# Expert weights in one ring of nine places, and token rows fetched by index lists and transposed, in a four-layer diffusion backbone with mixtures of experts

## The reference

```
def moe(h, router_w, router_b, wg, wu, wd):
    x = h.reshape(B * T, D)
    scores = sigmoid(x @ router_w)
    ...                                   # group-limited top 2 of 16 per token
    combine = einsum('nk,nke->ne', w, one_hot(idx, N_EXPERTS))
    hid = silu(einsum('nd,edf->nef', x, wg)) * einsum('nd,edf->nef', x, wu)
    y = einsum('nef,efd->nd', hid * combine[..., None], wd)
```

## Time and profile before

| | us |
|---|---|
| median of 3 runs | 1986.24 |
| lowest and highest | 1983.18, 1988.86 |
| the profiled execution | 1988.12 |
| its span, first to last instruction | 1986.3 |

### The profile page before, as it was taken

The page is one execution under the profiler, slowest core; times in us unless marked ns, Lnnn a source line. Parts: engine busy times, 40 slices in busy tenths (PEclk is TensorE's granted clock), DMA queues, the critical chain, the costliest instruction groups (busy, mean ns, idle before and its releaser), DMA issues.

```text
span 1986.3 us, 22833 instructions
## 1 busy us (share of the span) xinstructions
PE 1845.2 (93%) x9280; PEld 1115.4 (56%) x9280; DVE 482.3 (24%) x1240; ACT 385.8 (19%) x801; POOL 12.3 (1%) x24
## 2 busy tenths in 40 slices
PE   4988999999999969999999997999999969999986
PEld 2656644545735858745445565844554748444543
DVE  0132511104300341411112434321112143311102
ACT  1132200003102660200002223200002142000002
POOL 1000000000000000000000000000000000000000
PEclk8998999999998988999999998999999989999988
DMA  9992599996997332579998884559999445599960
GB/s 328 350 401 80 212 397 427 428 419 242 356 359 259 117 122 91 215 311 428 428 427 311 321 292 170 215 216 425 428 429 401 140 193 211 233 424 429 427 265 22
DMA packets 126142, 593.34 MB, mean 299 GB/s; under 512 B 8008, under 2 KB 15312, under 8 KB 101088
## 3 DMA queue, kind: packets, MB, share of 16 engines
q1 hardware_dynamic: 115728, 585.12, 74.0%
q10 hardware_dynamic: 9840, 6.51, 1.1%
q0 software_dynamic: 480, 0.39, 0.1%
HBM read 587.28 MB, written 4.73 MB: 298 GB/s over the span
## 4 chain that ended last, share of the span: by engine, by line
PE 70%; DMA 18%; DVE 5%; ACT 4%; issue 2%; ACTq 1%; SPq 0%; DVEq 0%
PE PS L865 23%; PE PS L1358 18%; DMA ring<-in_moe_wu 16%; PE PS L1337 7%; PE PS L1369 7%; PE PS L894 3%; PE PS L914 2%; PE PS L1317 1%; DMA ring<-in_attn_w_qkv 1%; DMA ring<-in_w_mod 1%; PE PS L932 1%; ACT arena L594 1%; DVE RS L1495 1%; PE PS L1254 1%; PE PS L1322 1%
## 5 line engine op out<-in xcount | busy, mean ns | idle before, releaser
L1358 PE MATMUL PS<-ring,arena 128*64 128x512 f32 x1312 | 353.0, 595 | 4.8 <-DMA ring<-in_moe_wu 3.1
L1337 PE MATMUL PS<-arena 128*128 128x128 f32 (+3 forms) x1584 | 252.1, 317 | 10.8 <-ACT arena L800 4.4
L1337 PEld LDWEIGHTS PS<-arena 128*128 128x128 f32 (+1 forms) x1584 | 222.7, 195 | 52.5 <-issue 25.0
L800 ACT ACTIVATE arena<-PS 128x512 f32<-128x512 f32 (+2 forms) x131 | 71.3, 545 | 873.2 <-PE PS L1369 359.3
L865 PE MATMUL PS<-HS,ring 128*128 128x256 f32 x1024 | 233.8, 386 | 3.5 <-DVE HS L1565 1.6
L1369 PE MATMUL PS<-ring,arena 128*64 128x512 f32 x1024 | 226.8, 595 | 3.4 <-DVE arena L1822 3.4
L865 PEld LDWEIGHTS PS<-HS,ring 128*128 128x128 f32 x1024 | 194.8, 193 | 39.0 <-issue 10.0
L1358 PEld LDWEIGHTS PS<-ring,arena 128*64 128x64 f32 x1312 | 114.4, 137 | 159.6 <-issue 158.4
L1841 DVE TENSOR_TENSOR arena<-arena,PS 128x512 f32<-128x512 f32 x32 | 33.5, 1047 | 556.6 <-PE PS L1358 556.6
L865 PE MATMUL PS<-arena,ring 128*128 128x256 f32 (+1 forms) x672 | 147.6, 381 | 2.7 <-ACT arena L608 1.5
L1369 PEld LDWEIGHTS PS<-ring,arena 128*64 128x64 f32 x1024 | 70.7, 137 | 135.7 <-issue 127.9
(11 more groups left out here) (309 smaller groups left out, 1393.8 us busy)
## 6 DMA issues: line engine op xcount, KB each, us to landing
ring<-in_moe_wd SPq DMA_DIRECT2D x64, 2048.0 KB, 12.2
ring<-in_moe_wu SPq DMA_DIRECT2D x49, 2048.0 KB, 22.1
ring<-in_w_mod SPq DMA_DIRECT2D x48, 2048.0 KB, 16.1
ring<-in_moe_wg SPq DMA_DIRECT2D x33, 2048.0 KB, 19.7
arena<-in_moe_wg SPq DMA_DIRECT2D x32, 2048.0 KB, 20.8
HS<-in_moe_wu SPq DMA_DIRECT2D x16, 2048.0 KB, 28.4
ring<-in_mlstm_w_in SPq DMA_DIRECT2D x12, 2048.0 KB, 8.8
ring<-in_attn_w_qkv SPq DMA_DIRECT2D x6, 2048.0 KB, 20.1
```

The costliest lines, as they stand in the source:

```text
L800: A(dst, src, func).then_inc(S(sem), 1)
L1337: return mm(out, rows, onehot, start=first, stop=final, skip_group_check=True)
L1358: ins = mm(PS[64 * e:64 * e + 64, b, :], XG[:, k, 64 * e:64 * e + 64], w[:, k], start=(k == 0), stop=(k == KD - 1))
```

## The change

Places. The nine places (six of the ring, three of EXTRA) are now one first-in first-out ring for the experts' chunks: `plan_slots` gives each chunk its place, SLOT, and the chunk that was there before, BEHIND. Chunk q of a layer (0 to 47) goes to the place of chunk q - 9 and waits for its use. Chunks 3 to 8 are loaded into `ring` during the mixer; chunks 0 to 2 go to the spare places in arena and HS when the mixer's result is there. The mixers' chunks stay in the ring of six.

Rows. Once the tokens are turned into HT, ScalarE writes HT to HBM (HR, "token_rows", 256 x 1024). VectorE compares the ranks with the 64 places for pairs 1 to 7 at once (`onehot`), and 14 matmuls of one column (`slot_id`, between the two up products of pair 0) multiply that by the token numbers: a list of 128 token numbers for each pair, IDX. GpSimd fetches the rows of each pair by its list with an indirect DMA from HR into HT[:, p % 2], where HT is now a buffer of two; TensorE transposes them (`turn_x`, 8 transposes) where it multiplied. The token numbers are kept less 300 (`tid`) and 300 is added to the sum, so a place without a token has the number 300, which is out of bounds (255 is the last row): its row is not fetched. Pair 0 keeps the product gather. After the gather of pair 7 SP reads HR back into HT for the overflow's gather, and the mixers wait for that (semaphore back).

TensorE's loop is written out, the one-hot blocks PB are made for pair 0 and the overflow alone, and the semaphores of the overflow are merged into three.

```
+SPARE = 3
+def plan_slots():
+    slot, behind, count, last, loads, ring = [], [], [], {}, {}, 0
+    for n, (kind, l, _) in enumerate(CHUNKS):
+        q = n - POS["wg", l, 0] if kind in ("wg", "wu", "wd") else None
+        if q is not None and q < SPARE:
+            at = RING + q
+        elif q is not None and q >= RING + SPARE:
+            at = slot[n - RING - SPARE]
+        else:
+            at, ring = ring % RING, ring + 1
...
# SP
-                for j in range(6):
-                    load(n + j)
+                for q in range(SPARE, SPARE + RING):
+                    load(n + q)
                 sp.wait_ge(S("x"), KD * (2 * l + 2))
...
-                for j in range(6):
-                    if j == 2:
+                for q in range(SPARE):
+                    if q == SPARE - 1:
                         sp.wait_ge(S("ht"), 4 * (l + 1))
-                    weight(j, 1, 1, 0)
-                with sp.Fori(1, NPAIR // 2) as i:
-                    for par in range(2):
-                        for j in range(6):
-                            weight(j, 2 * i + par, par, i)
+                    load(n + q)
+                for q in range(SPARE + RING, 3 * NE):
+                    load(n + q)
                 n += 3 * NE
+                sp.wait_ge(S("gather"), 2 * NPAIR * (l + 1))
+                for s in range(2):
+                    sp.dma_start(HT[:, s], HR[P * s:P * s + P]).then_inc(S("back"), 16)
# GpSimd
+            def rows(l):
+                pool.wait_ge(S("idx"), l + 1)
+                pool.wait_ge(S("rows"), 32 * (l + 1))
+                for p in range(1, NPAIR):
+                    pool.wait_ge(S("gather"), 2 * NPAIR * l + 2 * max(p - 1, 1))
+                    pool.indirect_dma_start(HT[:, p % 2], None, HR, bass.IndirectOffsetOnAxis(IDX[:, p:p + 1], 0),
+                                            bounds_check=N2 - 1, oob_is_err=False).then_inc(S(f"slot_rows{p % 2}"), 16)
# ScalarE, after the copies of the turned tokens
+                    if b % 2:
+                        load(HR[P * (b // 2):P * (b // 2) + P], HT[:, b // 2], "rows")
# TensorE
+                def turn_x(banks, par, sem):
+                    for k in range(KD):
+                        ins = tp(bank(banks[k // 4], P * (k % 4), P * (k % 4) + P), HT[:, par, P * k:P * k + P], ident)
+                def slot_id():
+                    pe.wait_ge(S("onehot"), 2 * (l + 1))
+                    for p in range(1, NPAIR):
+                        for s in range(2):
+                            ins = mm(bank(3, p, p + 1), OH[:, s, p].rearrange("t y n -> t (y n)"), c_("tid")[:, s:s + 1], start=(s == 0), stop=(s == 1))
...
                         turn_w(here[1], "turn_w")
-                        gather(there, "gather")
+                        pe.wait_ge(S(f"slot_rows{1 - par}"), 8 * i + (48 * l + 8 if par else 64 * l + 16))
+                        turn_x(there, 1 - par, "gather")
# VectorE, after the weights of pair 1, and after the table EXI
+                onehot(0)
+                onehot(1)
...
+                v.wait_ge(S("slot_id"), l + 1)
+                idf = RT[:, 480:480 + NPAIR - 1]
+                go(ts(idf, bank(3, 1, NPAIR), 300.0, None, ALU.add))
+                go(v.tensor_copy(IDX[:, 1:NPAIR], idf), "idx")
```

More of the change, by code:

```diff
@@ L146 @@
 POS = {chunk: n for n, chunk in enumerate(CHUNKS)}
+SPARE = 3
[9 more added lines that the diff above has]
+            at, ring = ring % RING, ring + 1
+        slot.append(at)
+        behind.append(last.get(at))
+        loads[at] = loads.get(at, 0) + 1
+        count.append(loads[at])
+        last[at] = n
+    return slot, behind, count
+SLOT, BEHIND, LOADS = plan_slots()
 WARM = (8, 8, 3, 1)
@@ L417, in load @@
                     sp.wait_ge(S("load_x"), 32)
-                if n >= RING:
-                    wait(sp, *used(n - RING))
-                sp.dma_start(slot_view(kind, n % RING), src_of(kind, l, c)).then_inc(S(f"landed{n % RING}"), 16)
+                if BEHIND[n] is not None:
+                    wait(sp, *used(BEHIND[n]))
+                sp.dma_start(slot_view(kind, SLOT[n]), src_of(kind, l, c)).then_inc(S(f"landed{SLOT[n]}"), 16)
             n = 0
@@ L462, in _ @@
                 with sp.If(nx > 0):
-                    wait(sp, *used(n - 12))
-                    wait(sp, *used(n - 11))
-                    wait(sp, *used(n - 6))
+                    for j in range(3):
+                        wait(sp, *used(n - RING - SPARE + j))
                     with sp.Fori(0, nx) as i:
@@ L820, in moe @@
                 wts(n0, 0, 2)
-                pair(n0, 0)
+                pair(n0, 0, first=True)
                 pair(n0 + 1, 1)
@@ L842, in _ @@
                 affine(2 * l, l, 0)
+                wait(act, "back", 32 * l)
                 (lambda: attention(l // 3, l), mlstm, gla)[l % 3]()
@@ L848, in _ @@
             norm(2 * DEPTH)
+            act.wait_ge(S("back"), 32 * DEPTH)
             for k in range(KD):
@@ L1909, in moe @@
+                        v.wait_ge(S("x_a"), x_step(before, i, "x_silu"))
+                        tt(by_k(HID[0:64]), row(SG[0:64]), row(PS[0:64, 5]), ALU.mult).then_inc(S("x_v"), 1)
+                        v.wait_ge(S("x_v"), x_step(before, i, "x_hid"))
+                        v.wait_ge(S("x_t"), x_step(before, i, "x_turn_h"))
+                        copy(HTS[:, :, 0:64], bank(6).rearrange("p (f t) -> p f t", f=4)[:, :, 0:64], "x_v", x_step(before, i, "x_hts"))
                 v.wait_ge(S("x_scatter"), before + nx)
@@ L1914, in _ @@
                 norm(2 * l, l, 0)
+                wait(v, "back", 32 * l)
                 (lambda: attention(l // 3, l), mlstm, gla)[l % 3]()
```

150 lines of the change are left out of this document (78 added, 72 removed).

## The result

The changed kernel takes 1956.36 us, the median of four runs (1947.04 to 1965.17). The kernel before, run beside it, takes 1984.71 us. The ratio is 0.9857, with a 95% interval of 0.9822 to 0.9891: 28 us, or 1.4%, faster. The prediction said 1945 us, with 1930 to 1998 as its range and 0.76 for faster by over 0.3%. Sign and range held; of the 41 us that it forecast, 28 came.

A forecast was written before the change was run, and what follows sets the result against it. TensorE and transfers were taken as nearly equal bounds, transfers deciding after the change: wu of pair 7 at 193.1 + 4.5 = 197.6, plus 19.14, gives 216.7 against 226.97 us a MoE; four times 10.3 saves 41, giving 1945 us, range 1930 to 1998.

The forecast's parts named there:

- TensorE's pair: MoE pairs: eight transposes replace 16 gather matmuls, saving 2.79 us, so a pair takes 25.84 us of TensorE instead of 28.63.
- The bound: Each MoE: transfers, not TensorE, set the end, 216.7 us against 208.1 + s (s the pair 0 stall).
- The list: Between pair 0's two up products: fourteen one-column products, 28 records, take 3.2 us of TensorE.
- Rival (c): TensorE's clock halves after waits in the last pairs; 5.7 us lost in each layer, 1968 us; chance 0.10.
- The waits on used places: Weight chunks waiting for ring places in pair 0 don't interrupt the stream; the next two are asked for at 17.1 us.
- The rows of pair 1: First indirect DMA in pair 0: lands 16.3 to 20.8 us after the first up product starts; TensorE wants it at 19.0.
- The stall of 1 us: TensorE's wait in pair 0 for pair 1's rows: 0 to 1.8 us, taken as 1, with up to 5 kept.
- The bytes: Gathered rows in the seven fetching pairs take 0.64 us of the DMA engines a gather, 4.5 us a layer.
- The break-even point of 2.1 us: DMA engine time per gather at which the MoE stays at 226.97 us; above it the kernel loses.
- Rival (b): A gather takes more DMA engine time than its bytes; at 3.5 us, 2025 us; chance 0.22, 0.14 of it slower.
- rival (e): Gathers cost nothing because the DMA engines fit them in: 212.2 us a MoE, 1927 us in all; chance 0.05.
- From wu of pair 7 to the end: From the last wu's landing to the end of the last down product: 19.14 us, as before the change.

The follow-up runs named there:

- e1: The kernel before with the new ring of nine places alone, every pair still gathered by the product; ratio to before 0.9935.
- e2: Rows fetched by index list and transposed as in the changed kernel, but weights in the old places and order; ratio to before 1.0124.
- e8: The changed kernel with the list's 28 fp32 products made 64 columns wide instead of one; ratio to before 0.9854.
- e5: e4 with one move: in pair 0 the rows of pair 1 are turned behind both downs; ratio to before 0.9811, run again 0.9833.
- e4: The changed kernel with the list's 14 one-column products in bf16, one record each; ratio to before 0.9881.
- e6: The changed kernel with all gathers issued but every index out of bounds, so no row is fetched; ratio to before 0.9819.
- e7: The changed kernel with the rows of pairs 2 to 7 fetched twice; ratio to before 0.9984.

## Why the prediction was right, and by how much it missed

**TensorE's pair.** Forecast 25.84 us, measured 25.93 (251.26 to 277.19 in layer 0). Sixteen products out, eight transposes in, nothing else changed. Right.

**The bound.** Forecast that the stream sets the end of every MoE, with waits of 2 to 3 us ahead of the second up product of the last pairs. Measured up to 2.7 us, 25 us for wu in all and 2.3 for wg; e1 and e2 show the two bounds apart. Right.

**The list.** Forecast 3.2 us for its records, measured 3.84 in layer 0. The step that failed is what stands behind it: the sum put the second up product at 6.95 us and so its end at 17.1. It ended at 19.0 (layers 1 and 2) or 20.7 (0 and 3), because one-column products were followed by half clock. Rival (c) had half clock only behind waits; here it came behind products that keep TensorE busy by the page. The three waits that rival (c) was read from were on VectorE and ScalarE, none on DMA. The Trainium skill (TensorE: Matmul & The Clock Gate, HAM oscillation) tells of half clock behind waits on DMA; the 231 to 237 window of the changed kernel, beside the one of e8, shows it with no wait at all.

**The waits on used places.** Forecast that they do not interrupt the stream, since the chunk behind the second up product would be asked for at 17.1 when the first two had just passed. At 19 to 20.7 they had passed long before, and the stream stood partly idle. That is the 2.3 us a layer between the changed kernel and e5, and it is the largest term missed. It follows from the step above. In layers 0 and 3 of e8, where the list takes 3.3 us and no half clock follows in pair 0, the chunk goes out at 17.4, and wu of pair 7 comes at 198.7, near the 198.3 of e5: there the forecast was nearly right.

**The rows of pair 1.** Forecast: landed between 16.3 and 20.8 us after the start, wanted at 19.0. In e4, where TensorE does not come late, they are there at 21.1 (240.14 less 219.02). The indirect DMA is issued at 232.93 in the changed kernel, 12.3 us after the start and not 10.6, and it lands 9.0 us after that, where the sum had 5.7 to 10.2. So it is the issue that comes late: the list is ready at 11.4, and GpSimd issues 0.9 us behind it. The stall of 1 us was a little low: e8, with a list of 3.3 us at full clock, is nearly the case of the sum, and there it is 1.2 to 1.9 (the 4.5 us of e4 stand behind a list that is shorter by over 3 us). In the changed kernel the wait is 0.4 us at most, since the half clock made TensorE late as well.

**The bytes.** Forecast 0.64 us a gather, measured 0.65 to 0.73 (0.42 and 0.92 in e6 and e7 before the gap and the weights moved ahead are counted). The break-even point of 2.1 us was never near. Rival (b) falls by this, and rival (e) by e7.

**From wu of pair 7 to the end.** Forecast 19.14. Measured 19.1 in layers 1 and 2 and 20.6 and 20.7 in 0 and 3, at half clock behind a wait of 2.7 us: rival (c) came true at a price of 1.5 to 1.6 us in two layers of four, not 5.7 in each.

**The sum again.** 197.6 forecast for wu of pair 7; plus 2.3 for the gap and 0.6 for dearer gathers is 200.5, and 200.6 was measured. The 0.6 is what e5 has above the forecast when its gap is closed (191.2 less 186.1 less 4.5); it is put down to the gathers here, and no run takes it apart. Plus 19.1 and 0.7 for the clock is 220.4; the mean is 220.5. So the 15 us a run that are missing from the MoE (3.8 a layer) have their names. Of the 41 us, 25 came from the MoE. The other 3 of the 28 lie outside it, where the forecast had nothing, within what a run varies by, and count as luck.

## What to carry to other kernels

Where two bounds lie close together, cost a change that eases one of them with the load it puts on the other, and expect its halves to be worth less alone than together. When an engine is sped up ahead of a wait, ask first what arrives next: here the fast list only showed the late rows, and it took a second move, of the reader of those rows behind work that does not need them, to turn it into time. And look at the clock behind a row of products with one column, not only behind waits.

## What the runs showed of the hardware

- 28 fp32 records with one column took 3.8 us (layer 0), 0.137 each, and were followed, with no wait between, by some 6 us at a granted clock of 0.50 in two layers and some 3 in the two others; 28 with 64 columns took 3.3 us and were not. 14 bf16 records with one column took 0.4 us in all, and were not either. The second mixer of the changed kernel has the same: 32 fp32 records with one column, 3.8 us, and a mean granted clock of 0.74 over the 6 us behind them.
- In the changed kernel an indirect DMA of 128 rows of 4 KB, about half of them out of bounds, landed 7.7 us after its issue at best, 10.8 in the middle and 12.1 at worst, on engines that were full with other transfers (up to 16.4 in e5). In e6, where no row is fetched, it took 7.2 to 11.7 all the same. In e2 the weights come later. This is the window of e2's layer 0 in which its first gather is issued, and the landing of the first three in that layer (3.4 us is the first, the other two found the engines partly busy):

```profile
228.90:235.00 6.10, 6.10 (x30) 3.96 (x31) 0.99 (x7) 1.88 (x2) 1.42 (x2) 0.63 0.00 0
```

```profile
DMA to landing us min/median/max: 3.4/4.2/5.6
```

  So it is the other transfers, not the rows' own bytes, that make a landing late. The Trainium skill (DMA: Bandwidth & Descriptors, Anatomy of one DMA) has 2.0 us plus the bytes over 436 GB/s, which gives an estimate of 2.6 us for 0.27 MB; the 3.4 us on idle engines are 0.8 above it, and on full engines the trace has three to six times as much.
- Rows out of bounds are not fetched, but their packets are sent: 4512 packets in GpSimd's queue whether 8.02 or 0.41 MB came with them.
- The same wait of 2.70 us ahead of the same product was followed by half clock in two layers and by full clock in the two others, in the same layers in both executions of e5. In e8 a wait of 1.2 us was followed by half clock, and one of 1.9 us was not.
